# Feed-forward rounds of a hybrid decoder layer: the order of six VectorE instructions at the start of each round

## The reference, cut to what matters

```python
h2 = rms_norm(x, norm_ffn_w)
g, u = jnp.split(h2 @ w_ffn_in, 2, axis=-1)
gp = jnp.concatenate([conv_buf.astype(g.dtype), g], axis=1)
gc = conv_b + gp[:, 0:T] * conv_w[0] + gp[:, 1:T + 1] * conv_w[1] + gp[:, 2:T + 2] * conv_w[2]
x = x + (jax.nn.silu(gc) * u) @ w_down
```

## Time and profile before

| | |
|---|---|
| median of 3 runs | 2416.53 us (2414.05 to 2416.75) |
| profiled execution | 2419.16 us, its span 2417.1 us |
| TensorE busy in the span | 2331.3 us (96%) |
| VectorE, ScalarE, GpSimd busy | 1589.5, 910.3, 922.5 us |
| mean granted TensorE clock | 0.985 of full speed |
| group 0 of the feed-forward part | from about 966 us to about 1375 us |

### The profile page before, as it was taken

The page is one execution under the profiler, slowest core; times in us unless marked ns, Lnnn a source line. Parts: engine busy times, 40 slices in busy tenths (PEclk is TensorE's granted clock), DMA queues, the critical chain, the costliest instruction groups (busy, mean ns, idle before and its releaser), DMA issues.

```text
span 2417.1 us, 36263 instructions
## 1 busy us (share of the span) xinstructions
PE 2331.3 (96%) x14278; PEld 2123.1 (88%) x14278; DVE 1589.5 (66%) x2554; ACT 910.3 (38%) x1556; POOL 922.5 (38%) x724
## 2 busy tenths in 40 slices
PE   7999889999988999899999999999999999999999
PEld 5899789999876788798888889999999899999997
DVE  4666726666665345777777876666667867667665
ACT  4555513433432233444333533332334333333331
POOL 4333202222211134654645543444444354354341
PEclk9999989999988999999999999999999999999999
DMA  7433211111123355422222442222223522222221
GB/s 265 159 123 119 83 55 49 65 63 49 56 90 116 131 187 184 165 88 88 88 88 88 162 164 70 70 70 70 70 70 108 206 75 70 70 70 70 70 70 70
DMA packets 150568, 243.30 MB, mean 101 GB/s; under 512 B 18241, under 2 KB 114205, under 8 KB 148333
## 3 DMA queue, kind: packets, MB, share of 16 engines
q1 hardware_dynamic: 150369, 240.93, 29.4%
q0 software_dynamic: 32, 0.07, 0.0%
HBM read 185.08 MB, written 56.84 MB: 100 GB/s over the span
## 4 chain that ended last, share of the span: by engine, by line
PE 59%; DVE 4%; POOL 3%; issue 2%; DMA 1%; ACT 0%; POOLq 0%; SPq 0%; DVEq 0%; ACTq 0%
PE bank L2498 11%; PE bank L2499 11%; PE bank L2500 11%; PE bank L113 9%; PE bank L114 8%; PE bank L115 8%; DMA late_b_raw<-in_w_ffn_in_dram 1%; DVE late_act_lo L2786 1%; POOL late_t L2979 1%; PE bank L2441 1%; DVE late_gp L2804 1%; DVE late_t_lo L2776 1%; PE bank L2450 0%; DVE late_t L2816 0%; DVE late_a_lo L2768 0%
## 5 line engine op out<-in xcount | busy, mean ns | idle before, releaser
L2804 DVE TENSOR_TENSOR late_gp<-bank,late_gp 128x384 f32<-128x384 f32 (+1 forms) x330 | 172.2, 522 | 323.5 <-PE bank L2500 323.3
L2498 PE MATMUL bank<-late_a_hi,late_b_hi 128*128 128x384 f32 (+1 forms) x1056 | 342.4, 324 | 6.6 <-DVE late_b_lo L2776 5.0
L2499 PE MATMUL bank<-late_a_lo,late_b_hi 128*128 128x384 f32 (+1 forms) x1056 | 341.3, 323 | 0.0
L2500 PE MATMUL bank<-late_a_hi,late_b_lo 128*128 128x384 f32 (+1 forms) x1056 | 340.2, 322 | 0.0
L2979 POOL TENSOR_TENSOR late_t<-late_t,late_gp 128x768 f32<-128x768 f32 (+1 forms) x66 | 132.2, 2021 | 499.4 <-DVE late_gp L2804 499.4
L113 PE MATMUL bank<-late_d_hi,late_act_hi 128*128 128x512 f32 (+1 forms) x724 | 283.1, 391 | 6.5 <-DVE late_acc L2830 4.7
L114 PE MATMUL bank<-late_d_lo,late_act_hi 128*128 128x512 f32 (+1 forms) x724 | 282.0, 390 | 0.0
L115 PE MATMUL bank<-late_d_hi,late_act_lo 128*128 128x512 f32 (+1 forms) x724 | 282.0, 390 | 0.0
L2498 PE MATMUL bank<-late_a_hi,late_t_hi 128*128 128x384 f32 (+1 forms) x792 | 259.9, 328 | 14.6 <-DVE late_gp L2804 11.9
L2830 DVE TENSOR_TENSOR late_acc<-bank,late_acc 128x512 f32<-128x512 f32 (+1 forms) x374 | 243.0, 680 | 34.6 <-PE bank L115 33.9
L2499 PE MATMUL bank<-late_a_lo,late_t_hi 128*128 128x384 f32 (+1 forms) x792 | 256.2, 324 | 0.0
(11 more groups left out here) (331 smaller groups left out, 5260.4 us busy)
## 6 DMA issues: line engine op xcount, KB each, us to landing
late_b_raw<-in_w_ffn_in_dram SPq DMA_DIRECT2D x66, 1024.0 KB, 5.1
late_d_raw<-in_w_down_dram SPq DMA_DIRECT2D x32, 1024.0 KB, 5.0
att_next_hh<-h_parts SPq DMA_DIRECT2D x16, 1024.0 KB, 4.9
late_a_raw<-h_parts SPq DMA_DIRECT2D x14, 768.0 KB, 6.1
att_x<-in_x_prompt_dram SPq DMA_DIRECT2D x16, 512.0 KB, 5.1
h_parts<-att_h_hi SPq DMA_DIRECT2D x16, 512.0 KB, 3.1
h_parts<-att_h_lo SPq DMA_DIRECT2D x16, 512.0 KB, 4.5
late_o<-mixed SPq DMA_DIRECT2D x16, 512.0 KB, 4.6
```

What stands on the lines that cost most here:

```text
L2498: nc.tensor.matmul(out, w_h, hi[:, c, :], start=first, stop=False, skip_group_check=True)
L2499: nc.tensor.matmul(out, w_h, lo[:, c, :], start=False, stop=False, skip_group_check=True)
L2500: ins_ = nc.tensor.matmul(out, w_l, hi[:, c, :], start=False, stop=last, skip_group_check=True)
L2804: nc.vector.tensor_tensor(dst, bk, src, ALU.add).then_inc(c_dve, 1)
```

## The change

In 30 of 33 rounds VectorE's first six instructions are put in another order. `split_act(p, 1)` now stands right behind `split_act(p, 0)`, with bank read 0 behind it; `split_d(p, 0)` goes from between the two activation differences to behind bank read 0, and `split_d(p, 1)` from behind bank read 0 to behind bank read 1. No instruction is added or taken away, and no other engine's order is touched.

```diff
             if p is not None:
                 split_act(p, 0)
-                if not turned:
-                    split_d(p, 0)
                 split_act(p, 1)
             combine(r, 0, 0)
             if turned:
                 split_a(G, S1)
             elif p is not None:
-                split_d(p, 1)
+                split_d(p, 0)
             combine(r, 0, 1)
             if turned:
                 split_a(G, A22)
+            elif p is not None:
+                split_d(p, 1)
             combine(r, 0, 2)
```

## The result

The change makes the kernel slower: 2434.91 us (median of 6 runs, 2429.41 to 2440.47) against 2416.41 us before (median of 6), ratio 1.0074 with a 95% interval of 1.006 to 1.0088. That is 18.5 us. I had forecast slower, with 2425 as the time and +8.5 us as the sum. The direction and the main mechanism are in the trace; the sum was less than half of it.

The account below looks back on a forecast made before the run. TensorE, busy 96% of the span, bounds the kernel. Group 0 +7.2, +6.5, -0.6 and -1.8, groups 1 and 2 -2.8: +8.5 us on 2419.16, 2427.7, or 2425 against the run median; range 2407 to 2439, forecast alone 2420 to 2432.

Parts of the forecast that it names:

- The gain at product 3: An earlier bank read 0 ends TensorE's stop at product 3, 0.95 us a round in group 0; 13.0 us at most overall.
- hitch: Around product 3 in groups 1 and 2, 0.14 us lost per round, 2.8 us in 20 rounds, to be won.
- Differences and sums keep each other out: VectorE's down-weight differences and GpSimd's weight sums exclude one another; whichever comes second waits for nearly all of the other.
- GpSimd first at the near tie: Group 0, second difference against second sum within 0.05 us: GpSimd first costs +0.8 us a round, +1.9 with two caught.
- Product 6 stops: In group 0 with GpSimd first, bank read 2 comes late for product 6: a new stop of 0.35 us.
- The catches in tap 1: Group 0's down phase: GpSimd's gate sums hold up VectorE's tap 1 instructions, about 1.1 us each, delaying item 5.
- two rounds with VectorE first: In two group 0 rounds the second difference precedes the second sum; three instructions caught, +3.25 us each, +6.5 together.
- Groups 1 and 2: Longer products leave room for the colliding differences and sums, so the gain of 2.8 us stands.
- the third rival: VectorE gets ahead of the second sum in all eight early-landing rounds of group 0: +21 us, 2437; chance 0.15.
- The first, the stop goes and nothing comes back: Product 3's stop goes without new costs: 13.0 us off, or 8 with some stops left, 2404 to 2409; chance 0.20.
- The fourth, down weights too late for their items: Down-weight differences come too late for down items; done by about 1048, items start at 1050: 2 us room, no time.

Follow-up runs that it names:

- experiment 3: Changed kernel, with group 0's next gate-weight load issued only after item 2 of the down phase, round 10 still early: 2414.23 us, ratio 0.9986.
- experiment 7: Changed kernel, with the gate load issued only after item 2 of the down phase in all ten rounds of group 0: 2411.56 us, ratio 0.9972.
- Experiment 4: Kernel before, with TensorE's item 5 waiting for addition 4 instead of addition 1 in ten down phases of group 0: 2460.0 us, ratio 1.0172.
- experiment 10: Kernel before with the new order only in groups 1 and 2, run once more in more rounds: 2415.94 us, ratio 0.9987.
- unclear first one: Kernel before with the new order only in groups 1 and 2, first measurement: 2417.12 us, ratio 0.9998.
- experiment 5: Kernel before, with the gate load issued only after item 2 of the down phase in the ten rounds of group 0: 2416.8 us, ratio 0.9992.
- experiment 9: Kernel before, with the new order only in groups 1 and 2 and the later gate load in group 0: 2413.9 us, ratio 0.9981.
- experiment 2: Kernel before with the new order only in group 0: 2439.55 us, ratio 1.0089.
- experiment 8: Experiment 7's kernel, but in group 0 the first down-weight difference precedes both activation differences and the second follows bank read 0: 2415.46 us, ratio 0.9987.

## Why the prediction was right, and where it was short

- *The gain at product 3.* Right in size: no stop in rounds 2 to 10, and groups 1 and 2 lose their hitch (45.83 instead of 45.96 us a round, forecast 0.14). A further 1.1 us, between the first two down phases of group 1, isn't tied to the order (see groups 1 and 2 below).
- *Differences and sums keep each other out; GpSimd first at the near tie.* Right in nine rounds of ten: 0.02 to 0.05 us apart, 2.33 to 2.36 us for the difference. Product 6 stops by 0.2 to 0.3 us (forecast 0.35), the sums end 0.32 us behind the phase's start (forecast 0.3). Nothing of this was visible as a wait before.
- *The catches in tap 1.* The mechanism was right (experiments 3 and 7), the weight wrong. I had worked out +0.8 us a round for one catch and +1.9 for two, and put six rounds at 1.2. Eight of ten rounds had two, one had three, one none: the second long instruction of tap 1 starts 5.38 to 5.41 us behind the phase's start, and the load lands at 5.2 to 5.4. (In rounds 1 and 8 VectorE's row even starts 0.01 or 0.02 us ahead of the sum's, and the instruction is held up all the same, 1293.38 against 1293.39 in round 8: at such a distance the starts in the rows don't say who goes first.) I could have worked that out: tap 1 began 3.56 us behind the start before, its second half is one long and one short instruction later, and I had the chain 0.85 us later. A round of this kind measured +1.6 us against 36.9 where the clock stayed up; I had +1.9 for it, so the price of two catches was right, and the count of them was the term that was too small. I had also counted two rounds with VectorE first at +3.25; one round, the fourth, had VectorE first, three catches and a stop of 4.0 us, and there it was the up-weight load, landing 1 us later than in the others, that moved the sums to 1.16 us behind the phase's start.
- *What the sum left out.* The lower clock behind the stops. It had no term. It comes in six rounds; at 1.7 us each (the granted clock of 0.83 over ten us, and the 40.2 to 40.3 against 38.3 to 38.6 us in the table) that is some 10 us, more than half of the loss. Experiment 4 shows that it belongs to the stop. Without it, the ten rounds cost about 16 us (eight at 1.6, round 4 at 3.5, round 2 at -0.3) where I had booked 13.1. So, as an estimate from these rows, 8.5 + 3 for the catches + 10 for the clock - 0.8 for groups 1 and 2 (below) - 1.8 for the earlier start of group 0 = 19, against the 18.5 measured.
- *Groups 1 and 2.* Right, with one part of it luck: -3.6 us by the trace, -3.1 by time (experiment 10, after an unclear first one), forecast -2.8. The rounds at issue give 2.5 us of the 3.6. The other 1.1 us are in the first down phase of group 1, in a round whose order wasn't changed. There the gate load comes near tap 1 too; before and after:

```profile
1397.70 1.29 POOL L2965 TENSOR_TENSOR late_t_raw<-late_b_raw 128x512 f32<-128x512 f32 x1 [3.93 <-DMA late_b_raw<-in_w_ffn_in_dram]
1397.82 3.95 DVE L2816 SCALAR_TENSOR_TENSOR late_t<-late_gp,late_cc,late_t 128x768 f32<-128x768 f32 x2
1402.43 0.50 PE L113 MATMUL bank<-late_d_hi,late_act_hi 128*128 128x512 f32 x1 [1.55 <-DVE late_acc L2830]
...
1419.89 2.98 DVE L2816 SCALAR_TENSOR_TENSOR late_t<-late_gp,late_cc,late_t 128x768 f32<-128x768 f32 x2
1420.10 1.96 POOL L2965 TENSOR_TENSOR late_t_raw<-late_b_raw 128x512 f32<-128x512 f32 x1 [4.26 <-DMA late_b_raw<-in_w_ffn_in_dram]
1423.53 0.50 PE L113 MATMUL bank<-late_d_hi,late_act_hi 128*128 128x512 f32 x1 [0.58 <-DVE late_acc L2830]
```

  Before, the sum starts first and both instructions of the tap are caught; after, the tap starts first and one is. It goes either way whatever the order: the trace of experiment 5, with the order of before, has the shorter stop (0.55 us), that of experiment 9, with the new order in groups 1 and 2, the longer one (1.68 us).
- *The rivals.* The measured time, 2435, lies within the stated 2407 to 2439, but outside the 2420 to 2432 of the forecast alone, and next to the 2437 of the third rival, VectorE first throughout. The trace has GpSimd first in nine rounds, so that rival is out as a mechanism: its number came about by the lower clock, of which neither had a term. The first, the stop goes and nothing comes back, is what the late load makes of the kernel. The fourth, down weights too late for their items, is out: TensorE waits for `late_d_lo` twice, 1.7 us in all, in both traces, each time in the first round of group 1 or 2.

Still open: why a stop of 2.1 to 2.5 us is followed by the lower clock in some rounds (9 of 17 in the traces of after and of experiments 2 and 4) and not in others, while each of the ten stops of 3.7 us and more in the traces was. Open too: how much of the loss the earlier first bank read causes, and how much the two differences among the sums.

## What to carry to other kernels

An instruction that is taken out from ahead of a critical one has to run somewhere; before you move it, write down which engine it can't run beside, and where that engine will be then. Look at the slack of the next serial chain as well: here 0.5 us of slack and a DMA landing some 0.1 us behind the chain were what held the old order together, and neither shows in a list of waits. When such a change loses, try the time at which the colliding load is issued before you give up the order: one more wait on SyncE turned +18.5 us into -6.8, of which some 3 us are the new order in groups 1 and 2, and the rest the late load and group 0.

## What the runs showed that I had not expected

- A stop of TensorE of little over 2 us can cost 1.5 to 1.7 us more than itself: 7 or 8 matmuls of 512 columns at a step of 0.43 instead of 0.23 us.
- A near tie of two engines can repeat in the same way through a trace: with 0.02 to 0.05 us between them GpSimd was first in nine of ten rounds (2.33 to 2.36 us for the difference). A tie with a DMA landing in it can't be counted on: the one in group 1 went one way in some traces and the other way in others, for 1.1 us.
- VectorE's idle time beside a busy GpSimd isn't free: a difference put into it (experiment 8) took 1.77 us, and the two activation halves behind it 2.87 instead of 2.14.
